# GLA's last token group: fine levels multiplied ahead of the coarse ones

## The reference, cut to what matters

```python
w = jnp.exp(jnp.where(causal[None, :, :, None, None], b[:, :, None] - b[:, None, :], -jnp.inf))
scores = jnp.einsum('bihd,bjhd,bijhd->bhij', qc, kc, w)
o = (jnp.einsum('bhij,bjhe->bihe', scores, vc) + jnp.einsum('bihd,bhde->bihe', qc * jnp.exp(b), s))
s = s * jnp.exp(b_last)[..., None] + jnp.einsum('bjhd,bjhe->bhde', kc * jnp.exp(b_last[:, None] - b), vc)
```

## Time and profile before

| What | Value |
|---|---|
| median of 3 runs | 2370.93 us (2370.62 to 2371.5) |
| the profiled execution, its own time | 2369.45 us |
| its span, first to last instruction | 2367.4 us |
| PE busy | 2348.8 us (99%) |
| DVE, ACT, POOL busy | 1299.5, 790.3, 1212.4 us |
| granted TensorE clock | 0.999 |
| GLA stage, from the first scores to the last | 1179 to 1520 us |

### The profile page before, as it was taken

One profiled execution on the slowest core, in us unless ns is written; L12 is line 12 of the kernel. 1 busy time (PEld: TensorE's weight loads), 2 busy tenths in 40 slices (PEclk: granted clock), 3 DMA queues, 4 the chain that ended last, 5 costly groups with the idle time before them and its releaser, 6 DMA issues. The chain is left out here.

```text
span 2367.4 us, 45305 instructions
## 1 busy us (share of the span) xinstructions
PE 2348.8 (99%) x17800; PEld 2303.7 (97%) x17800; DVE 1299.5 (55%) x2039; ACT 790.3 (33%) x1252; POOL 1212.4 (51%) x1439
## 2 busy tenths in 40 slices
PE   9999999999999999999999999999999999999998
PEld 9999899999999999999999999999999999999998
DVE  6863254345545545556676776633444544544566
ACT  4701442222222222232454565622223223223224
POOL 2554146465665766666211112355476566566681
PEclk9999999999999999999999999999999999999999
DMA  4223031111111111112211112131111111111112
GB/s 165 65 65 92 28 131 41 50 41 50 51 39 49 50 45 45 54 46 104 80 47 66 57 46 75 49 120 45 45 45 46 55 45 45 49 51 45 45 56 83
DMA packets 41676, 142.48 MB, mean 60 GB/s; under 512 B 6448, under 2 KB 10160, under 8 KB 40336
## 3 DMA queue, kind: packets, MB, share of 16 engines
q1 hardware_dynamic: 32768, 106.78, 13.8%
q10 hardware_dynamic: 8720, 33.01, 4.0%
HBM read 120.42 MB, written 14.88 MB: 57 GB/s over the span
## 5 line engine op out<-in xcount | busy, mean ns | idle before, releaser
L766 PE MATMUL PS<-RB,WH 128*128 128x384 f32 (+1 forms) x4320 | 1069.6, 329 | 0.0
L766 PE MATMUL PS<-RA,WH 128*128 128x272 f32 (+2 forms) x3520 | 768.8, 308 | 2.9 <-DVE RA L1960 0.8
L766 PEld LDWEIGHTS PS<-RB,WH 128*128 128x128 f32 x4320 | 759.8, 188 | 5.4 <-issue 2.3
L766 PE MATMUL PS<-RB,WL 128*128 128x384 f32 (+1 forms) x2208 | 720.9, 327 | 0.0
L653 POOL TENSOR_TENSOR WH<-WR,FEW 128x256 fp32r<-128x256 f32 x416 | 321.7, 804 | 584.5 <-PE PS L766 555.7
L766 PEld LDWEIGHTS PS<-RA,WH 128*128 128x128 f32 x3520 | 585.9, 188 | 11.2 <-issue 4.3
L766 PE MATMUL PS<-RA,WL 128*128 128x272 f32 (+2 forms) x1760 | 540.5, 307 | 0.0
L766 PEld LDWEIGHTS PS<-RB,WL 128*128 128x128 f32 x2208 | 414.5, 188 | 0.0
L657 POOL TENSOR_TENSOR WL<-WR,WH 128x256 fp32r<-128x256 f32 x416 | 368.6, 916 | 0.0
L766 PEld LDWEIGHTS PS<-RA,WL 128*128 128x128 f32 x1760 | 330.7, 188 | 0.0
L2061 DVE TENSOR_TENSOR X<-PS,X 128x544 f32<-128x544 f32 x280 | 202.5, 724 | 204.2 <-PE PS L766 204.2
(11 more groups left out here) (243 smaller groups left out, 2253.7 us busy)
## 6 DMA issues: line engine op xcount, KB each, us to landing
WR<-ws SPq DMA_DIRECT2D x189, 512.0 KB, 3.4
EB<-xT ACTq DMA_DIRECT2D x8, 544.0 KB, 5.4
x_spill<-X ACTq DMA_DIRECT2D x8, 544.0 KB, 2.7
EB<-x_spill ACTq DMA_DIRECT2D x8, 544.0 KB, 6.4
GA<-st_gla ACTq DMA_DIRECT2D x4, 1024.0 KB, 4.8
glas_o<-GA ACTq DMA_DIRECT2D x4, 1024.0 KB, 4.6
yT<-X SPq DMA_DIRECT2D x16, 208.0 KB, 1.9
X<-xT ACTq DMA_DIRECT2D x4, 544.0 KB, 6.0
```

The costliest lines, as they stand in the source:

```text
L766: return nc.tensor.matmul(out, lhsT, rhs, start=start, stop=stop, skip_group_check=True)
```

## The change

For e % 3 == 2 (group 2 of each head) turns 1 and 2 of `prepare` are arranged anew. `X1` and `XE1` move from turn 2 to the end of turn 1, behind `P`; `Q6` and `Q5` leave turn 1; turn 2 is `XE0 Q2 Q1 Q0 Q6`, then `B(4)`, then `Q5 Q4 Q3`. The wait of `Q0` for its exponential is rewritten, as its place among the `Q` items no longer gives the count. The same items are issued as before, with the same operands; PE's own order does not change.

```diff
@@ -223,6 +223,10 @@
     q = lambda *vs: [("Q", e, v) for v in vs]
     if turn == 0:
         return x(6, 5), x(4)
+    if e % 3 == 2:
+        if turn == 1:
+            return [("KD", e), ("DE", e)] + x(3, 2), [("P", e)] + x(1)
+        return [("XE", e, 0)] + q(2, 1, 0, 6), q(5, 4, 3)
     if turn == 1:
         return [("KD", e), ("DE", e)] + x(3, 2) + q(6), [("P", e)] + q(5)
     return x(1) + [("XE", e, 0)] + q(4, 3), q(2, 1, 0)
@@ -2577,7 +2581,7 @@
                                                                               gQ(h)[:, s:s + n]))
                     dve.wait_ge(psum_free, made(("k", h), g))
                     if v == 0:
-                        dve.wait_ge(x0_ready, nth("Q", e, v) // LEVELS)
+                        dve.wait_ge(x0_ready, e + 1)
                         V.tensor_tensor(right, right, qr, ALU.mult).then_inc(lev_ready, 1)
                     else:
                         dve.wait_ge(x_ready, exps(e, v))
```

## The result

| | before | changed |
|---|---|---|
| median of 17 runs each | 2371.5 us (2369.51 to 2372.91) | 2377.26 us (2374.2 to 2380.69) |
| the profiled execution, its own time | 2369.45 us | 2374.2 us |
| its span | 2367.4 us | 2372.2 us |
| mean granted clock | 0.999 in the profiled one | 0.997 in the profiled one, 0.994 to 0.996 in the other 16 |

The ratio is 1.0025, 95% interval 1.0018 to 1.0032: 5.8 us slower by the medians, over the 0.2% that can be told, and outside the predicted range (2369.0 to 2375.4). The profiled execution is the shortest of the 17, 4.75 us above the profiled one of before.

What follows compares the result with a forecast made beforehand. PE was taken to bound the kernel, busy 2348.8 of 2367.4 us. Delays of 0.40, 1.48 and 0.89 us in heads 0, 1 and 2 summed to 2.77 us on the 2370.93 us median: 2373.7 us, range 2369.0 to 2375.4.

Steps and rivals of the forecast that it cites:

- head 3's immunity: B of chunk 8 in head 3: PE starts it 8 us after chunk 5's output copy, so the delay costs nothing.
- 0.17 us of slack: Before B of chunk 8, heads 1 and 2: PE can go at 1313.76 and goes at 1313.93 in head 1.
- Head 0's term: B of chunk 8 in head 0: 0.40 us more work in turn 2, no slack, so PE loses 0.40 us.
- the one from waits to time: B of chunk 8, head 1: GN2 1.65 us late, less 0.17 us slack, moves PE by 1.48 us.
- The working of the lateness: DVE turn 2: Q0 waits for XE0, holding up the work behind it; GN2 1.65 us late in head 1, 1.06 in head 2.
- four products at 0.7 us end at 1304.3: DVE, head 1: Q2 and Q1 slowed by POOL's pass still fill the wait for XE0, so nothing was charged.
- The step that blamed X1's move: ACT, head 1: XE1 waits for X1, so the copy of chunk 5's keys and values starts 1.18 us late.
- The stall goes and nothing takes its place: Scores of chunk 8, heads 1 and 2: up to 3.1 us of PE time won, 2367.8 us; chance 0.15.
- Gain and loss cancel: ACT reaches XE0 earlier as products avoid POOL's pass in head 1; within 1 us of 2370.9; chance 0.14.
- Slower by more: POOL's pass slips onto Q0, Q6, Q5, Q4 in heads 1 and 2: 6.8 us slower, 2377.7 us; chance 0.05.
- My chance of 0.93 for no change: Whole kernel: no change means within about 0.2%, 4.7 us; slower had 0.05 and faster 0.02.

Runs made afterwards that it cites:

- turn 2 alone: Against the changed kernel: turn 1 as before with Q6 and Q5 in it, turn 2 X1 XE1 XE0 Q2 Q1 Q0, B(4), Q4 Q3; 2371.44 us, ratio 1.0001.
- five more copies: Kernel before, with ScalarE making the copy of chunk 5's output six times in heads 0 to 2, same values; 2381.86 us, ratio 1.0045.
- the kernel with the pass moved away: Changed kernel, with ScalarE rounding weights behind units 11 and 16 with the unit's second group, so POOL's pass comes after turn 2; 2379.33 us, ratio 1.0036.
- the third group: Last of three groups in which the twelve follow-up kernels were timed, each beside the kernel before, whose median there was 2371.36 us.

## Why the prediction was wrong, point by point

**The waits were nearly right.** I had 0.40, 1.48 and 0.89 us for heads 0, 1 and 2, and measured 0.42, 1.15 and 0.89 us. The waits themselves, forecast as 0.7, 1.9 and 1.9 us, are 0.91, 1.74 and 1.73 us. The place (B of chunk 8, for line 1873), the cause (VectorE late at GN2, everything behind it shifted, 0.17 us of slack) and head 3's immunity came as said. Head 1 is 0.33 us less because in the trace of before P started 0.49 us after the exponential it needs ended, in head 2 only 0.13 us; it is 0.10 us in the changed kernel. This is no accident of one execution: 0.48 us stands in head 1 also in the profiles of all five experiments that keep the old order of products and PE's own order, *turn 2 alone* has it in head 2, and every kernel with the new turn 1 has 0.10 us in both. I took P's start as fixed; why the new turn 1 shortens the pause stays open. Head 0's term was right at B and worth nothing in the time, as the pause behind it gave it back.

**The step that failed is the one from waits to time:** "a delay of 1.65 us therefore moves PE by 1.65 - 0.17 = 1.48 us". It assumed that a wait of PE costs its own length, so the sum has no term for the clock. The table of the kernel before gave 0.999 for the clock, and I did not ask what keeps it there. The profiled run lost 2.98 us in two falls of the clock behind such waits (falls like the one in head 0 come in the old order too, as the last section says, so this pair of profiles charges the change with more than its share there). The median shows more: 5.8 us less 2.5 us of waits leaves 3.3 us, or 4.2 us if the pause gave back 0.85 us there too. The kernel with five more copies shows that longer waits alone bring more falls.

**The working of the lateness was half right.** I had DVE idle for over 1 us in front of Q0 in heads 1 and 2. It was 0.29 us in head 1 and nothing in head 2, as three of the four fine products take 0.85 us each beside POOL's pass and fill that time. I had named this ("four products at 0.7 us end at 1304.3") and yet forecast the idle time. XE0 and the collisions nearly tie in head 1, so the sum came near (GN2 1.32 us late for 1.65, in head 2 1.06 us as forecast). That is luck: the wait that I priced is hardly there, and the collisions that I took nothing for fill its place. The Trainium skill's rule on the shared port ("SBUF — State Buffer", "SBUF: two separate sides") is borne out: these products read two SBUF tensors and take 0.85 us beside the pass, 0.31 us without it, and 0.32 us in the kernel with the pass moved away.

**The step that blamed X1's move had the wrong cause.** The move did put ScalarE's copy of chunk 5's keys 1.18 us later after P, as I wrote, but with X1 put back GN2 gained only 0.1 us in heads 1 and 2 and lost 0.5 us in head 0, and the waits rose from 4.4 to 5.0 us. What costs is Q6 and Q5: Q6 was free behind the wait for P, and both now stand between Q0 and GN2.

**The rivals.** "The stall goes and nothing takes its place" fell by the table of waits; its 3.1 us were also too much, as the same table of the kernel before has 1.4 us in all four waits. "Gain and loss cancel" describes the kernel with turn 2 alone (1.0001). "Slower by more" (0.05) had the right side and about the size, by another mechanism: POOL's pass did not slip behind XE0 in the changed kernel, though it did what that rival says when it was moved by hand. My chance of 0.93 for no change rested on the sizes of the waits alone.

## What to carry to other kernels

Moving products ahead of others on an engine that has no idle time there only chooses which consumer waits: list every copy that stands behind the reordered work, and find its slack, before counting the gain. Work that sits in front of a wait of its engine is free, and moving it behind the wait is a cost. In this kernel, with TensorE 99% busy, waits of about 2 us cost nearly twice their length (three of them, 5.7 us more than before, cost 10.2 us), so price such a wait with the clock. And look for a pause behind a wait that is there anyway: it can give the wait back.

## What the runs showed of the hardware that was not expected

The granted clock fell to 0.5 behind PE waits of 0.5 to 2.8 us, or behind the pause alone, and the falls came in two sizes: 1.71 or 3.4 us of clock not granted. Over the fourteen profiles (before, changed and the twelve kernels), heads 1 and 2 had 10 falls in the 14 cases where PE had waited 1.3 us or more around B of chunk 8, and 1 fall in the 14 cases with less than 1 us. In head 0 the size of the wait does not sort them: 8 of 14 profiles have a fall there, two of the three kernels without any wait for the copy among them (with pauses of 0.9 and 1.6 us), and one with a wait of 0.89 us and a pause of 0.28 us has none. So head 0 is hit in the old order too, and what the longer waits add is the falls of heads 1 and 2.

The kernel before lies in such steps too: of the 33 runs in the third group, six at 0.999 (2368.9 to 2369.7 us), seventeen at 0.998 and ten at 0.997 (2372.4 to 2373.5 us). So its profiled run, the one I argued from, showed it at its best, and a single trace can hide a cost that most executions pay. What sets whether a given wait is followed by a fall was not tried.
